# The 64 bytes under xn: moving activations against the split weights in SBUF

## What is computed

```
first block, per layer:
  x = x + 0.5 * swiglu(rms_norm(x), w_gu[1024 x 5632], w_down[2816 x 1024])
  x = x + mixer(rms_norm(x), w_in[1024 x 5192], ...)   # gated spatial product, top-64 attention, w_pa, w_pb, w_out
  x = x + 0.5 * swiglu(rms_norm(x), w_gu, w_down)
second block, per layer:
  h = mixer_2(rms_norm(x), w_in[1024 x 3592], ...)     # gated delta rule, windowed attention, w_out
  x = x + rms_norm(h)
  h = (gelu(conv3(rms_norm(x) @ up)[gate]) * conv3(...)[val]) @ down
  x = x + rms_norm(h)
```

## Time and profile before

| | us |
|---|---|
| median of 3 runs | 2171.36 (2168.77 to 2172.14) |
| the profiled execution, its own time | 2171.4 |
| its span in the trace | 2169.4 |
| TensorE, matmuls in flight | 1997.0 (92%) |
| VectorE busy | 1223.9 (56%) |
| ScalarE busy | 998.3 (46%) |
| GpSimd busy | 657.7 (30%) |
| mean granted clock of TensorE | 0.951 |

### The profile page before, as it was taken

One profiled execution on the slowest core, in us unless ns is written; L12 is line 12 of the kernel. 1 busy time (PEld: TensorE's weight loads), 2 busy tenths in 40 slices (PEclk: granted clock), 3 DMA queues, 4 the chain that ended last, 5 costly groups with the idle time before them and its releaser, 6 DMA issues.

```text
span 2169.4 us, 41175 instructions
## 1 busy us (share of the span) xinstructions
PE 1997.0 (92%) x15758; PEld 1947.2 (90%) x15758; DVE 1223.9 (56%) x1478; ACT 998.3 (46%) x1306; POOL 657.7 (30%) x595
## 2 busy tenths in 40 slices
PE   6999979999999999898999999978999889869997
PEld 6999979999999999898999988967999789769997
DVE  4545475665455554755654575526664564456665
ACT  5434444544344344454543464444544463445543
POOL 4651201246317610302365113313330006122320
PEclk9999889999999998999999989988999889989999
DMA  6545433455455444334454532203545322124544
GB/s 227 193 140 191 160 104 130 147 184 193 143 188 198 171 161 177 109 141 136 167 202 144 189 122 93 95 32 105 173 157 173 117 97 98 39 75 139 174 157 153
DMA packets 49213, 314.26 MB, mean 145 GB/s; under 512 B 5712, under 2 KB 6864, under 8 KB 19920
## 3 DMA queue, kind: packets, MB, share of 16 engines
q1 hardware_dynamic: 48960, 311.09, 41.8%
q10 hardware_dynamic: 144, 1.69, 0.2%
HBM read 311.71 MB, written 1.05 MB: 144 GB/s over the span
## 4 chain that ended last, share of the span: by engine, by line
PE 63%; issue 18%; DVE 8%; ACT 6%; POOL 4%; DMA 1%; ACTq 1%; DVEq 0%; SPq 0%; POOLq 0%
PE ps L542 17%; PE ps L544 17%; PE ps L543 17%; PE ps L857 3%; DVE conv L1875 2%; PE ps L547 2%; PE ps L548 2%; PE ps L549 2%; ACT conv L1160 2%; ACT w_hi L1109 2%; DVE w_lo L1567 1%; DMA raw<-in_in_dram 1%; POOL m L2197 1%; DVE v L2073 1%; POOL rope_tmp L2161 1%
## 5 line engine op out<-in xcount | busy, mean ns | idle before, releaser
L1567 DVE TENSOR_TENSOR w_lo<-raw,w_hi 128x2048 fp32r<-128x2048 f32 (+1 forms) x322 | 707.1, 2197 | 405.1 <-ACT w_hi L1109 403.6
L542 PE MATMUL ps<-xn,w_hi 128*128 128x256 f32 x2688 | 783.1, 291 | 44.1 <-DVE w_lo L1567 15.6
L543 PE MATMUL ps<-xn,w_hi 128*128 128x256 f32 x2688 | 772.0, 287 | 0.0
L544 PE MATMUL ps<-xn,w_lo 128*128 128x256 f32 x2688 | 771.3, 287 | 0.0
L1109 ACT ACTIVATE w_hi<-raw 128x2048 fp32r<-128x2048 f32 (+1 forms) x322 | 561.9, 1746 | 115.3 <-DMA raw<-in_down_dram 74.8
L542 PEld LDWEIGHTS ps<-xn,w_hi 128*128 128x128 f32 x2688 | 527.8, 196 | 56.8 <-issue 39.7
L543 PEld LDWEIGHTS ps<-xn,w_hi 128*128 128x128 f32 x2688 | 528.1, 196 | 0.6 <-issue 0.5
L544 PEld LDWEIGHTS ps<-xn,w_lo 128*128 128x128 f32 x2688 | 527.5, 196 | 0.0
L542 PE MATMUL ps<-h,w_hi 128*128 128x256 f32 x1056 | 297.2, 281 | 9.7 <-DVE conv L1875 5.1
L544 PE MATMUL ps<-h,w_lo 128*128 128x256 f32 x1056 | 295.4, 280 | 0.0
L543 PE MATMUL ps<-h,w_hi 128*128 128x256 f32 x1056 | 295.3, 280 | 0.0
(11 more groups left out here) (310 smaller groups left out, 2716.5 us busy)
## 6 DMA issues: line engine op xcount, KB each, us to landing
raw<-in_gu_dram SPq DMA_DIRECT2D x132, 1024.0 KB, 4.8
raw<-in_in_dram SPq DMA_DIRECT2D x70, 1024.0 KB, 4.9
raw<-in_down_dram SPq DMA_DIRECT2D x96, 704.0 KB, 4.0
raw<-in_out_dram SPq DMA_DIRECT2D x16, 1024.0 KB, 4.8
raw<-in_pb_dram SPq DMA_DIRECT2D x4, 1024.0 KB, 4.8
raw<-in_pa_dram SPq DMA_DIRECT2D x4, 1024.0 KB, 4.9
tables_all<-in_tables_dram ACTq DMA_DIRECT2D x1, 1648.0 KB, 7.0
rows<-in_rows_dram SPq DMA_DIRECT2D x2, 768.0 KB, 6.8
```

Source lines behind the costliest of these rows:

```text
L542: pe.matmul(out, w, xh, start=first, stop=False)
L543: pe.matmul(out, w, xl, start=False, stop=False)
L544: return pe.matmul(out, wl, xh, start=False, stop=last)
L1567: dve.tensor_tensor(w_lo[:, r, 0:elems], raw[:, k % RAW_RING, 0:elems], w_hi[:, r, 0:elems], ALU.subtract).then_inc(lo.sem, 1)
```

## The change

Two constants of the SBUF layout change:

```
-XN_AT = X_AT + KC * T * 4
+XN_AT = X_AT + KC * T * 4 + 64
 FIXED_AT = XN_AT + 2 * KC * T * 4
...
-    area = (cursor[0] + 63) // 64 * 64
+    area = (cursor[0] + 63) // 128 * 128 + 64
```

## The result

The changed kernel takes 2144.84 us (median of 4 runs, 2138.66 to 2146.99) against 2170.66 us for the kernel before (4 runs). The ratio is 0.9878, 95% interval 0.9858 to 0.9897: 22 to 31 us faster, about 26. The forecast was 13 us. The profiled execution took 2143.15 us, its span is 2141.2 us, 28.2 us less than before, at nearly the same mean clock (0.952 against 0.951).

What follows compares the result with a forecast made beforehand. The prediction took the start-to-start step of TensorE's matmuls to bound first-block gate-up stages; 9.1 us there plus 3.9 us in input projections made 13.0 us off 2171.36, so 2158 us, range 2136 to 2173.

Steps and rivals of the forecast that it cites:

- if h moves: Sign of a wrong forecast: windows with h should still hold 427 matmuls in 50 us, so h's pitch stays.
- the likeliest case: The forecast of 2158 us with its own span, 2151 to 2163 us; chance 0.57.
- the pitch of xn: Start-to-start step of matmuls with xn at full clock: from 120.0 to 117.8 ns, 2.2 ns less each.
- The first rival: The position of xn does not set the pitch, which stays at 120: 2171 us, chance 0.20.
- part (2): The activation area moves by 128 bytes, from 143,808 to 143,936, and stays 64 off a multiple of 128: 0 us.
- The coarser modulus: Rival: a modulus above 128 counts, slowing h, m, y, yb and ya to 120 ns: +9.5 us, 2181 us; chance 0.10 for slower.
- 113.5 as a bound for xn: Rival: the 113.5 ns pitch of ya in the first layer becomes xn's rule: 38 us, 2133 us; chance 0.13.
- The term for xn: Matmuls with xn at full clock gain 2.2 ns each, in first-block gate-up and input projections: 13.0 us.
- the gate-up stages: Four gate-up stages of the first block: 4,128 matmuls by 2.2 ns, nothing hiding them: 9.1 us.
- the projections: Input projections: 2,930 matmuls at full clock, at most 6.4 us, taken times 0.6 for TensorE's waits: 3.9 us.
- The second block's gate-up: Two gate-up stages where TensorE waits for conv at every pair: 0 us, 4.6 us if it did pay.
- Tables and writers of xn: Fixed tables moved by 64 (transposes, 0.4 or 1.1 us) and ScalarE and VectorE writes of xn (0.5 us): each taken as 0.

Runs made afterwards that it cites:

- the best kernel: xn and the area both placed 192 bytes above the weights modulo 256, against the kernel before: 2130.95 us, ratio 0.9831; a second run took 2127.89 us.

## Why the prediction was wrong

**The way was right, the size was half.** 13 us were forecast and 26 measured; 2144.84 lies in the range. The prediction had named "if h moves" as a sign of being wrong, and h moved. (The upper end of the likeliest case, 2163, should be 2171.4 - 9.1 = 2162.)

**What bounds the kernel, and the pitch of xn: right.** The windows went from 752 to 767 matmuls (766 was forecast), the median from 283 to 279 ns. The first rival, that the position of xn does nothing, is out. The rule of two independent read ports ("TensorE: Matmul & The Clock Gate" in the Trainium skill, section "Step-by-step: what each phase is for") does not describe this pair of streams: the step of one instruction is 113.3, 117.8 or 120.0 ns by the place of its operands. The 109 ns that the prediction took from the section "Back-to-back issue gap" of the same page of the Trainium skill are an isolated matmul's, without room for a weight load, as the section says; nothing in the sum rested on them.

**The step that failed is part (2): "For the modulus of 128 this part changes nothing: cost 0".** The area's 128 bytes are worth about 10 us of the 26 (ratio 0.9953 alone). The coarser modulus stood among the rivals, but with the wrong sign and with "nothing at all points to it". The earlier trace rows did point to it: tiles at one placement had shown 113.5 and 118.2. I took 113.5 as a bound for xn, and never asked what it would be worth for h, m and y, which were the ones that moved. In the trace after, 73% of their matmuls go at 113.3. Less the 192 with yb and ya of the first layer, which did so before, (4,320 x 0.73 - 192) x 4.4 ns is 13 us, against 10 measured for the area alone with an interval of 4 to 16.

**The term for xn** was 9.1 us for the gate-up stages and 3.9 for the projections, 13.0 together; xn alone measured 0.7% of 2170, 15 us, with an interval of 10 to 20. The gate-up stages gave 6.9 us, in the trace of the changed kernel and in that of xn alone. Three of them gave 1.8 to 2.3 us each, the size forecast. The first gave 0.7, but it takes 125.3 us in the trace before and 126.8 in the one with everything moved by 64, at the same pitch, so such a stage is known to 1.5 us and no better.

**The projections gave more:** 7.9 us in the trace of xn alone, though one of their four stretches differs by 2 us between two traces of one pitch. One reason can be seen. Where xn is stationary (L547 to L549) the weights stream past it, and the distance is counted the other way: 64 becomes 192, the good one. Here are such products before and after:

```profile
244.00:250.00 6.00, 6.00 (x52) 1.00 0.38 153
...
847.00:853.00 6.00, 6.00 (x55) 1.00 0.32 134
```

In the trace after, half of these products at full clock are at 113.3 ns; in the kernel with the weights moved, where the distance so counted is 64, fewer than one in ten are. I had given them the same 2.2 ns. The half is some 650 matmuls by 4.5 ns, at most 3 us; the rest of the surplus stays open.

**The clock at m** was in no term, and gave 3 us of the profiled 28 (rows in the first section). It belongs to the part put at 0 too, since it came only with the area at distance 192, in 7 of 10 stages; its cause stays open.

**The second block's gate-up: right at 0.** This is ScalarE after the change, the counterpart of the earlier trace rows. Columns: start us, duration us:

```profile
1530.45 0.42 ACT L1544 ACTIVATE silu_gate<-conv 128x256 f32<-128x256 f32 x1 [2.99 <-DVE conv L1875]
1530.77 1.90 ACT L1109 ACTIVATE w_hi<-raw 128x2048 fp32r<-128x2048 f32 x1
...
1536.69 0.42 ACT L1544 ACTIVATE silu_gate<-conv 128x256 f32<-128x256 f32 x1 [3.11 <-DVE conv L1875]
```

The beat is 6.24 us, against 6.25 before, and TensorE's wait grew instead. In the stage from 1469 us on, its first 20 us left out as in the trace before, the wait for conv is now

```profile
PE ps L542 <- DVE conv L1875: 5.4, 15, 0.5
```

(total us, times, longest) and was 3.1 us. With xn at distance 192 the stage still takes 139.0 us: none of the pitches tried shortens this stage.

**Tables and writers of xn: 0, as taken.** After the change, against 504, 484 and 275 ns in the earlier trace rows:

```profile
L1146 ACT ACTIVATE xn<-x,gains 128x256 fp32r<-128x256 f32 x32 | 15.4, 503 | 55.9 <-DVE x L1834 26.3 <-DVE x L1608 25.5 <-DMA eps<-in_eps_dram 4.2
L1580 DVE SCALAR_TENSOR_TENSOR xn<-x,gains,xn 128x256 fp32r<-128x256 f32 x32 | 14.9, 484 | 25.4 <-ACT xn L1146 25.4
L672 PE MATMUL ps<-tables_all,roped 128*128 128x128 f32 x80 | 10.6, 275 | 0.7 <-POOL roped L2164 0.7
```

The step of the transposes is 109 ns before and after.

## What to carry to other kernels

When matmuls follow each other without a gap and each loads new weights, divide a window's length by its matmuls for every stage, and compare tiles of the same shape: a steady difference of 2% between them can be a matter of placement, which one constant in the layout tests. Here it paid where TensorE sets the time, and not at all in the two stages whose beat lies elsewhere. Read the granted clock of both windows before you call a shorter stage a shorter step. Look at the distance of the streamed tile from the loaded one, with a modulus coarser than the one that first explains the rows, and take a rare good value in the trace as a question of what brings it about, not as a mere bound.

## What the hardware showed

- Steady steps of an fp32r matmul of 128 x 128 by 256 with a new weight load each, at the 2.4 GHz level, by distance modulo 256: 0: 120.0 ns; 32: 116.9 or 117.7; 64: 117.8, rarely 113.3; 128: 118.6 to 118.9, or 120.0; 160: 117.4 to 118.6; 192: 113.3 or 117.8; 224: 118.6. (A window of 50 us gives them to 0.3 ns. 96 was not tried.)
- At distance 192 the step is drawn for a stage: the two traces of the changed kernel differ in which down stages have the short one, and so do the two of the best kernel. The kernel in which only the area had moved took 2148 to 2169 us; that the draw makes this spread fits its size (up to 19 us) but is not shown, since only one of its runs has a trace.
- At the 1.2 GHz level the step was about 213 ns at the distances 0, 64 and 192 alike (xn before, m before, xn with the weights moved).
- The short pitch leaves little below it. The few products of the second block that stream only 8 columns past a 128 x 128 tile of xn, each with a load of its own, follow one another at nearly the same pace. In the kernel before, start us and duration us, ten steps apart:

```profile
1725.81 0.25 PE L549 MATMUL ps<-ba_hi,xn 128*128 128x8 f32 x1
...
1726.93 0.25 PE L547 MATMUL ps<-ba_hi,xn 128*128 128x8 f32 x1
```

  That is 112 ns for 8 columns, against 113.3 to 120.0 for 256, and 213 ns at the 1.2 GHz level, as with 256. So 248 columns fewer shorten the best step by less than 2 ns; that the weight load sets it is an inference, which no run tested.
- What stays open: which two reads meet. That w_lo alone and the weights alone change the step fits a weight load meeting the stream of a matmul, but no run separated the two, and h with w_lo moved does not fit the plain mean. Nor is it known what draws the step at distance 192, or why the third gate-up stage always drew the long one; a placement that always gives 113.3 would be worth some further microseconds, and was not found.
